# Six conditioning units computed on VectorE inside the feed-forward, weight slabs split two at a time there, pairs of PSUM banks that start even

## The reference

```python
for i in range(DEPTH_2):
    mod = (cond @ ada_w[i] + ada_b[i])[:, None, :]
    shift1, scale1, gate1, shift2, scale2, gate2 = jnp.split(mod, 6, axis=-1)
    h = rmsnorm(x, norm1_g[i]) * (1.0 + scale1) + shift1
    ...
    x = x + gate1 * y
    h = rmsnorm(x, norm2_g[i]) * (1.0 + scale2) + shift2
    x = x + gate2 * swiglu(h, f_w_in[i], f_w_out[i])
```

## Time and profile before

| what | us |
|---|---|
| median of 3 runs (1325.82 to 1327.03) | 1325.92 |
| the profiled execution | 1325.81 |
| its span (first to last instruction) | 1324.0 |
| PE busy in the span | 1137.3 (86%) |
| DVE busy | 633.5 (48%) |
| ACT busy | 547.1 (41%) |

### The profile page before, as it was taken

The page is one execution under the profiler, slowest core; times in us unless marked ns, Lnnn a source line. Parts: engine busy times, 40 slices in busy tenths (PEclk is TensorE's granted clock), DMA queues, the critical chain, the costliest instruction groups (busy, mean ns, idle before and its releaser), DMA issues.

```text
span 1324.0 us, 20070 instructions
## 1 busy us (share of the span) xinstructions
PE 1137.3 (86%) x8573; PEld 843.4 (64%) x8573; DVE 633.5 (48%) x1331; ACT 547.1 (41%) x1185; POOL 0.2 (0%) x4
## 2 busy tenths in 40 slices
PE   6999999867665765756799989999999989999997
PEld 4777667534343442424467758788887758888886
DVE  4565765111111011101175765776666765776665
ACT  4554554111011111101155664666654654666653
POOL 0000000000000000000000000000000000000000
PEclk9999999999798897879999999999999999999999
DMA  9996947999999999999998645654546555655400
GB/s 390 421 425 246 386 160 296 429 427 426 427 425 426 427 426 425 428 427 426 426 403 327 253 192 195 251 191 191 191 159 249 226 224 199 246 191 191 191 32 32
DMA packets 29703, 397.37 MB, mean 300 GB/s; under 512 B 3496, under 2 KB 4904, under 8 KB 5416
## 3 DMA queue, kind: packets, MB, share of 16 engines
q1 hardware_dynamic: 29176, 395.72, 73.5%
q10 hardware_dynamic: 432, 0.30, 0.1%
HBM read 394.97 MB, written 1.05 MB: 299 GB/s over the span
## 4 chain that ended last, share of the span: by engine, by line
PE 61%; DMA 23%; DVE 9%; ACT 6%; issue 1%; SPq 0%; DVEq 0%; ACTq 0%
PE ps L1140 16%; DMA ring<-in_w13b 12%; PE ps L1141 8%; DMA mem<-in_w13b 6%; PE ps L1132 5%; PE ps L1134 5%; PE ps L1133 5%; PE ps L1173 4%; DMA ring<-in_w 4%; PE ps L1643 3%; ACT mem L1815 3%; PE ps L1603 2%; DVE memr L2309 2%; PE ps L1698 2%; ACT memr L1815 2%; DVE mem L2309 2%
## 5 line engine op out<-in xcount | busy, mean ns | idle before, releaser
L2309 DVE TENSOR_TENSOR memr<-ring,memr 128x512 fp32r<-128x512 f32 x432 | 294.2, 690 | 207.2 <-ACT memr L1815 201.2
L1815 ACT ACTIVATE memr<-ring 128x512 fp32r<-128x512 f32 x432 | 266.0, 628 | 197.4 <-PE ps L1141 99.2
L1140 PE MATMUL ps<-memr 128*128 128x512 f32 x952 | 339.1, 399 | 2.8 <-DVE memr L2315 1.8
L1815 ACT ACTIVATE mem<-ps 128x512 f32<-128x512 f32 (+5 forms) x307 | 128.4, 439 | 402.1 <-PE ps L1643 231.6
L1141 PE MATMUL ps<-memr 128*128 128x256 f32 x952 | 267.3, 281 | 0.0
L1140 PEld LDWEIGHTS ps<-memr 128*128 128x128 f32 x952 | 178.9, 188 | 47.9 <-DVE memr L2315 5.9
L1132 PE MATMUL ps<-memr 128*128 128x256 f32 (+2 forms) x504 | 178.8, 355 | 6.8 <-DVE memr L2309 3.9
L1141 PEld LDWEIGHTS ps<-memr 128*128 128x128 f32 x952 | 179.9, 189 | 1.7
L1134 PE MATMUL ps<-memr 128*128 128x256 f32 (+2 forms) x504 | 165.4, 328 | 0.0
L1133 PE MATMUL ps<-memr 128*128 128x256 f32 (+2 forms) x504 | 165.2, 328 | 0.0
L2309 DVE TENSOR_TENSOR mem<-mem,ps 128x512 f32<-128x512 f32 (+1 forms) x76 | 43.5, 572 | 243.1 <-ACT mem L1815 243.0
(11 more groups left out here) (180 smaller groups left out, 1086.2 us busy)
## 6 DMA issues: line engine op xcount, KB each, us to landing
ring<-in_wpk SPq DMA_DIRECT2D x89, 2048.0 KB, 8.2
ring<-in_w13a SPq DMA_DIRECT2D x17, 2048.0 KB, 45.3
mem<-in_w13b SPq DMA_DIRECT2D x16, 2048.0 KB, 45.3
ring<-in_w SPq DMA_DIRECT2D x16, 2048.0 KB, 45.7
ring<-in_w13b SPq DMA_DIRECT2D x16, 2048.0 KB, 43.6
mem<-in_w13a SPq DMA_DIRECT2D x15, 2048.0 KB, 45.3
mem<-in_w SPq DMA_DIRECT2D x15, 2048.0 KB, 46.3
mem<-in_wpk SPq DMA_DIRECT2D x1, 2048.0 KB, 11.2
```

Source lines behind the costliest of these rows:

```text
L1140: te.matmul(ps[:, 0:512], a[0], b[1], start=start, stop=False)
L1815: return self.e.activation(out, src, f, **k)
L2309: return self.e.tensor_tensor(out, a, b, op)
```

## The change

1. Six units, `TURNED` = (1,10), (2,2), (2,3), (2,6), (2,7), (2,8), are taken off PE. Their weights are laid out turned on the host, so that `turned_chunk` computes 128 columns of the unit in one DVE operation: a scalar_tensor_tensor of 128 x 1024 that multiplies the weights with `m.cond` (silu(c) in all partitions) and writes the sum over each row into `m.mcol`. Four chunks make a unit, `turned_end` adds the bias. The generator `turned_units` is put into `p.side` ahead of layer 2's feed-forward and issues one chunk every five slab steps: 24 chunks over 116 of the 132 steps of that feed-forward.
2. `spread_cond` makes `m.cond` once among the experts: eight small PE matmuls and two ACT copies. `m.cond` takes the place of some constants and of `rowb[:, 0]`, so from group 4 on only z = 1 is used.
3. The six units are loaded between the units of layer 2's feed-forward (`TURNED_AT`), no more in the attention phases. Group 7 is now (2,4), (2,5); it is complete before layer 3 begins and is copied in the third step of its modulation.
4. In both feed-forwards `p.at_once = 2` during the 11 blocks: `stage` waits until two of the four places are free, and splits two slabs with one ACT and one DVE operation of 1024 columns.
5. `take_pair` only takes pairs of banks that start with an even one.
6. `warm(9)` is added between the first two modulation units.

```diff
@@ -95,8 +95,10 @@
        ((0, 10), (0, 11), (1, 0), (1, 1), (1, 2), (1, 3)),
-       ((1, 4), (1, 5), (1, 6), (1, 7)), ((1, 8), (1, 9), (1, 10), (2, 2), (2, 3)), ((1, 11), (2, 0), (2, 1)),
-       ((2, 4), (2, 5), (2, 6), (2, 7), (2, 8)), ((2, 9),), ((2, 10), (2, 11)))
+       ((1, 4), (1, 5), (1, 6), (1, 7)), ((1, 8), (1, 9)), ((1, 11), (2, 0), (2, 1)),
+       ((2, 4), (2, 5)), ((2, 9),), ((2, 10), (2, 11)))
+TURNED_AT = (0, 2, 4, 6, 8, 11)
+TURNED = ((1, 10), (2, 2), (2, 3), (2, 6), (2, 7), (2, 8))
 ADA_AT = {u: (g, r) for g, units in enumerate(ADA) for r, u in enumerate(units)}
@@ -246,12 +248,13 @@
         self.cols = sb("cols", [128, CN])
-        self.cst = sb("cst", [128, KN])
+        self.cst = sb("cst", [128, KN + 1024])
         self.w40 = sb("w40", [128, NK, 40])
         self.am = sb("am", [128, 3, 2, 8])
-        self.rowb = sb("rowb", [128, 2, 512])
+        self.rowb = self.cst[:, KN:KN + 1024].rearrange("p (a b) -> p a b", a=2)
+        self.cond = self.cst[:, KN - 512:KN + 512]
         self.csb = sb("csb", [128, 2, NK, 31 + ADA_MOST])
@@ -410,14 +413,16 @@
     mixed((U_AQKV, 8), ada(1, 4), (U_AQKV + 2, 8), ada(1, 5), (U_AQKV + 4, 8), ada(1, 6), ada(1, 7),
-          (U_AQKV + 1, 8), ada(1, 8), (U_AQKV + 3, 8), ada(2, 2), (U_AQKV + 5, 8), ada(2, 3),
-          (U_AWO, 8), ada(1, 9), ada(1, 10), (U_AWO + 1, 8), ada(1, 11), ada(2, 0), ada(2, 1))
+          (U_AQKV + 1, 8), ada(1, 8), (U_AQKV + 3, 8), (U_AQKV + 5, 8),
+          (U_AWO, 8), ada(1, 9), (U_AWO + 1, 8), ada(1, 11), ada(2, 0), ada(2, 1))
     for i in range(2):
-        mixed(*[(U_FIN + 11 * i + n, 8) for n in range(11)],
-              *[(U_FOUT + 6 * i + n, 8 if n < 5 else 4) for n in range(6)])
+        for n in range(17):
+            packed(*((U_FIN + 11 * i + n, 8) if n < 11 else (U_FOUT + 6 * i + n - 11, 8 if n < 16 else 4)))
+            if i == 0 and n in TURNED_AT:
+                packed(*ada(*TURNED[TURNED_AT.index(n)]))
         if i == 0:
-            mixed(ada(2, 4), ada(2, 5), (U_BQKV, 8), (U_BQKV + 2, 8), (U_BQKV + 1, 8), (U_BWO, 8), ada(2, 6), ada(2, 7),
-                  ada(2, 8), (U_BWO + 1, 8), ada(2, 9), ada(2, 10), ada(2, 11))
+            mixed(ada(2, 4), ada(2, 5), (U_BQKV, 8), (U_BQKV + 2, 8), (U_BQKV + 1, 8), (U_BWO, 8),
+                  (U_BWO + 1, 8), ada(2, 9), ada(2, 10), ada(2, 11))
     return units, dense, moe_last
@@ -479,15 +485,15 @@
     def stage(self, most=NSP):
-        most += self.made
-        while not self.hold and self.made < min(len(self.slabs), most) and self.made < self.spent + NSP:
+        most = min(len(self.slabs), most + self.made)
+        while not self.hold and self.made + self.at_once <= min(most, self.spent + NSP):
             n, j = self.slabs[self.made]
             k = self.made
-            self.made += 1
+            self.made += self.at_once
             self.split(k, n, j)
-            if j == self.dense[n][-1]:
+            if j + self.at_once - 1 == self.dense[n][-1]:
                 self.load_unit(self.slot_of[n], (self.s.dve_low, k))
@@ -550,7 +556,9 @@
             g, last = self.ada_made.pop(0)
-            z = self.ada_n % 2
+            z = 1 if g >= 4 else self.ada_n % 2
+            if g >= 4:
+                self.ada_close(True)
             self.ada_n += 1
@@ -568,6 +576,22 @@
+    def turned_units(self):
+        for i, n in TURNED:
+            u = self.unit()
+            self.in_use.remove(u)
+            for c in range(4):
+                self.turned_chunk(i, n, c, u)
+                if c < 3:
+                    for _ in range(5):
+                        yield
+            self.turned_end(i, n)
+            self.ada_done.add((i, n))
+            self.load_unit(self.slot_of[u], (self.s.dve_mod, (i, n)))
+            for _ in range(5):
+                yield
@@ -755,6 +779,7 @@
         self.extra_end()
+        self.spread_cond()
         self.next_gather(GUARD + 1)
@@ -881,16 +906,13 @@
         qk_unit("q11", 2, 0.125, m.qT1, 1, self.a_free)
-        self.ada_unit(2, 2)
         qk_unit("k11", 0, 1.0, m.kT1, 1, self.turned("q10"))
-        self.ada_unit(2, 3)
         self.side.append(self.paced(at, [4, 0, 0, 0]))
         self.ada_unit(1, 9)
-        self.ada_unit(1, 10)
         self.side.append(self.paced(at, [0] * 9))
@@ -911,10 +933,7 @@
         last = self.last
-        self.ada_mm(2, 6)
         self.drain()
-        self.ada_copy()
-        self.ada_close(True)
         last_q = self.chain(*[rope("q21", m.qst2[1][:, tt, :], 4, 0, tt, 4 + tt) for tt in range(2)])
@@ -924,10 +943,6 @@
             next(last_q, None)
-            if step in (1, 4):
-                self.ada_unit(2, 7 if step == 1 else 8)
-            if step == 6:
-                self.ada_close(True)
         self.side.append(self.paced(at, [0] * 8))
@@ -945,6 +960,7 @@
     p.ada_copy()
+    p.warm(9)
     p.ada_mm(0, 2)
@@ -1062,6 +1078,9 @@
         p.modulate_x(i, 1, ("m", i), {3: p.ada_copy})
+        if i == 1:
+            p.side.append(p.turned_units())
+        p.at_once = 2
         for n in range(11):
@@ -1070,6 +1089,7 @@
         p.h2_free = [(s.pe_slab, p.last)]
+        p.at_once = 1
         p.norm_open(("f", i))
@@ -1105,7 +1125,7 @@
         at = {b[0]: j for j, b in enumerate(self.banks)}
-        i = min((i for i in range(7) if i in at and i + 1 in at), key=lambda i: (max(at[i], at[i + 1]), i))
+        i = min((i for i in range(0, 8, 2) if i in at and i + 1 in at), key=lambda i: (max(at[i], at[i + 1]), i))
         freed = [dict(self.banks)[i + z] for z in range(2)]
@@ -1172,6 +1192,20 @@
+    def spread_cond(self):
+        te, w, s, m = self.e, self.w, self.s, self.m
+        for h in range(2):
+            b = self.take(("cond", h))
+            w.wait_ge(s.dve_cond, 1)
+            w.wait_ge(s.ld_c1, "c1")
+            self.ready(b)
+            for k in range(4):
+                c = m.csb[:, 1, 4 * h + k, ADA_MOST - 1:ADA_MOST].to_broadcast([128, 128])
+                r = te.matmul(b.ps[:, 128 * k:128 * k + 128], c, m.ident, start=True, stop=True)
+            r.then_inc(*s.pe_ada.up(("cond", h)))
+            self.give(("cond", h), (s.act_row, ("cond", h)))
@@ -1836,11 +1870,21 @@
         w.wait_ge(self.ring(n), n)
-        for f in self.split_free[k % NSP]:
-            w.wait_ge(*f)
-        self.act(m.sp[:, k % NSP, 0, :], self.slot(n)[:, 512 * j:512 * j + 512]).then_inc(*s.act_high.up(k))
+        z, a = k % NSP, self.at_once
+        for q in range(a):
+            for f in self.split_free[z + q]:
+                w.wait_ge(*f)
+        self.act(m.sp[:, z:z + a, 0, :], self.slot(n)[:, 512 * j:512 * (j + a)].rearrange("p (a n) -> p a n", a=a)
+                 ).then_inc(*s.act_high.up(*range(k, k + a)))
+    def spread_cond(self):
+        w, s, m = self.w, self.s, self.m
+        for h in range(2):
+            w.wait_ge(s.pe_ada, ("cond", h))
+            self.act(m.cond[:, 512 * h:512 * h + 512], m.of(("cond", h))[:, :]).then_inc(*s.act_row.up(("cond", h)))
+        self.row_free = [(), ()]
@@ -2331,10 +2375,10 @@
         w, s, m = self.w, self.s, self.m
-        z = k % NSP
+        z, a = k % NSP, self.at_once
         w.wait_ge(s.act_high, k)
-        self.tt(m.sp[:, z, 1, :], self.slot(n)[:, 512 * j:512 * j + 512], m.sp[:, z, 0, :], ALU.subtract
-                ).then_inc(*s.dve_low.up(k))
+        self.tt(m.sp[:, z:z + a, 1, :], self.slot(n)[:, 512 * j:512 * (j + a)].rearrange("p (a n) -> p a n", a=a),
+                m.sp[:, z:z + a, 0, :], ALU.subtract).then_inc(*s.dve_low.up(*range(k, k + a)))
@@ -2351,6 +2395,20 @@
+    def turned_chunk(self, i, n, c, u):
+        w, s, m = self.w, self.s, self.m
+        v = self.slot(u)[:, 1024 * c:1024 * c + 1024]
+        w.wait_ge(self.ring(u), u)
+        w.wait_ge(s.act_row, ("cond", 1))
+        self.e.scalar_tensor_tensor(out=v, in0=v, scalar=1.0, in1=m.cond, op0=ALU.mult, op1=ALU.mult,
+                                    accum_out=m.mcol[:, i, 4 * n + c:4 * n + c + 1]).then_inc(*s.dve_mod.up(("chunk", i, n)))
+    def turned_end(self, i, n):
+        w, s, m = self.w, self.s, self.m
+        mc = m.mcol[:, i, 4 * n:4 * n + 4]
+        w.wait_ge(s.dve_mod, ("chunk", i, n))
+        self.tt(mc, mc, m.cols[:, C_ADA + 48 * i + 4 * n:C_ADA + 48 * i + 4 * n + 4], ALU.add).then_inc(*s.dve_mod.up((i, n)))
```

More of the change, by code:

```diff
@@ L48 @@
 K_ID, K_ONE, K_INV, K1 = 0, 128, 256, 320
-K_M3, K_MT, K_U, K_BD, K_HS, K_IO = 320, 704, 832, 960, 1088, 1600
-K_CA, K_SA, K_CRC, K_SRC = 1632, 1664, 1696, 1952
+K_M3, K_MT, K_U, K_BD, K_IO = 320, 704, 832, 960, 1088
+K_CA, K_SA, K_CRC, K_SRC, K_HS = 1120, 1152, 1184, 1440, 1696
 KN = 2208
@@ L440, in __init__ @@
         self.hold = False
+        self.at_once = 1
         self.side, self.jobs = [], []
@@ L697 @@
     first_loads = late_loads = cond = rope_tables = first_norm = pad_conv = nothing
-    ada_product = ada_row = ada_turn = ada_gain = nothing
+    ada_product = ada_row = ada_turn = ada_gain = turned_chunk = turned_end = spread_cond = nothing
```

(6 more changed lines are left out.)

## The result

The changed kernel takes 1357.33 us (median of 5), the kernel before 1325.82 in the same session: ratio 1.0238, 95% interval 1.0227 to 1.025. It is slower, as forecast, but by 31.5 us and not by 21.9, and 0.3 us beyond the end of the range.

What follows compares the result with a forecast made beforehand. PE was taken to set the pace in the feed-forwards, chains of waits in attention. Terms -7.8 + 0.5 - 0.4 + 21.0 + 2.5 + 0.8 + 5.3 = +21.9 on 1325.81 gave 1347.7 us, range 1334 to 1357.

Steps and rivals of the forecast that it cites:

- term 3: Slabs in pairs in both feed-forwards: +21.0 us for waits in the blocks, +2.5 at their starts, +0.8 for `norm_tables`.
- term 4: The 24 chunks on DVE in layer 2's feed-forward: 1.30 us each, four of them costly, +5.3 us in all.
- term 1: Six modulation units off PE, mostly in attention: -7.8 us, of which (2,2) and (2,3) 3.7 and (1,10) 1.8.
- the walk: Step-by-step timing of one feed-forward block's ACT and DVE queues with pairs: PE waits 0.40, then 0.66 us.
- Two slabs ahead are enough: Rival, feed-forward blocks: the waits and the chunks' costs vanish, so it ends faster at 1320.6 us; chance 0.10.
- That is 1.05 us a block: Added PE wait per block with pairs, for ten blocks in each of two layers: 21.0 us.
- Start of the feed-forward: First pair comes later behind modulation on ACT and DVE: 1.6 us in layer 2, 0.95 in layer 3, sum 2.5.
- layer 3's +0.95: At the start of layer 3's feed-forward, slab 4 as half of a pair comes 0.95 us later.
- The clock rival: Holes in PE's work in the blocks halve the clock for a tenth of 361 us: +36, 1384 us; chance 0.03.
- The six in `fold_out` [...] 0: Six of the 24 chunks fall into `fold_out`, meet single splits with 2.9 us in hand and cost 0.
- no gain in attention: Rival: in attention another wait takes the removed units' place, so 7.8 us is not gained, 1355.5 us; chance 0.10.
- Term 2: What moves: group 7's copy +0.5 us, loads under the feed-forward hidden, `spread_cond` 0, even bank pairs 0, `warm(9)` -0.4.

Runs made afterwards that it cites:

- Experiment 2: The kernel before with only the slab pairs (`at_once`) in both feed-forwards, no chunks, odd bank pairs allowed; 1.0222 of the kernel before.
- 3: The changed kernel with two places still released together, but each split by its own ACT and DVE operation of 512 columns; 1.0032 of the kernel before.
- 4: The changed kernel with wide pairs, the later parts of `hidden` moved behind the pairs in the queues; 1331.43 us, 1.0036 of the kernel before.
- 5: The changed kernel with silu's table load moved from the first `hidden` to slab 5 of the first block; 1.0225 of the kernel before.
- 8: The changed kernel with single splits and units (2,2) and (2,3) back on PE, four turned units left; 0.9985 of the kernel before.
- 9: The changed kernel with single splits and without the nine idle matmuls `warm(9)` at the start; 0.9979 of the kernel before.
- experiment 11: The changed kernel with `hidden`'s later parts behind pairs, chunks after slabs 2 and 5, early table load, pairs from slab 4 of the first block; 1321.76 us, 0.9968.
- number 6: The changed kernel with the first chunk, and so all 24, three slab steps later; 1.0224 of the kernel before.

## Why the prediction was right in kind and short in size

The direction and the main mechanism were right; the sum was 9.6 us short. What failed are terms of the sum: the block in term 3 was put too low, the table load and the half clock were put at nothing, the last chunks of term 4 were put at nothing, and units (2,2) and (2,3) in term 1 were put at their full PE time. Experiment 2 shows that the pairs lose the time by themselves, 3 that the width of the operations and not the release in twos does it, 4 that it is the order in the two queues, and the steady block above follows the walk operation by operation. "Two slabs ahead are enough" is shown false for this order, and true for the order of 4 where there are no chunks (layer 3). Point by point:

- **Term 3, the block.** "That is 1.05 us a block" was mis-sized: 1.20 (12.49 against 11.29). The two waits are 0.45 and 0.60, in sum as walked (0.40 and 0.66). I left out that the first matmul pair after a wait takes 0.45 instead of 0.354, twice a block; 0.05 comes back as the pairs between the waits stand 0.347 apart. 20 blocks: 3.0 us too little.
- **Term 3, `hidden` at the first block.** The walk had no table load. Before, it lay in the 2.9 us of slack; with pairs it costs 0.8 in each layer, shown by 5: 1.6.
- **Start of the feed-forward.** The hole was as summed (0.51 + 1.6 = 2.1), and layer 3's +0.95 came as forecast. But I held the clock safe because attention keeps 1.00 with 79% busy; a busy share over 20 us says nothing about one hole. The clock rival came true for some 3 us, and that cost 1.6: this is the difference to number 5, which has the same hole at full clock. Whether such a hole brings the half clock differs from run to run, so this term is in part chance.
- **Term 4.** The chunk's 1.30 and its four costly places were right (extra 1.2 to 1.3 in those blocks), `norm_tables` too (0.8 in number 2). "The six in `fold_out` [...] 0" was wrong: the one after slab 2 of the second matrix delays the last product, and PE waits 0.88 at 981.62. The start of `fold_out` gives 1.1 in all.
- **Term 1.** (1,10) gave its 1.8 (1.9 from (1,9) to (2,1)). (2,2) and (2,3) gave 1.2 where I put 3.7, shown by 8: 2.5 too much. PE busy before and after a unit does not mean that nobody else needed the pause. This is the rival "no gain in attention" for two of the six units. Layer 3's attention came as forecast in sum, and I did not test its parts.
- **Term 2.** `warm(9)` gives nothing that can be told (9). Loads under the feed-forward and `spread_cond` left no trace in the stage times; they were not tried alone.

3.0 + 1.6 + 1.6 + 1.1 + 2.5 is 9.8; the miss is 9.6. All five go one way. The table load, the hole at the start and the late chunk are things that fit into slack before and not after; the restart behind a wait exists only with waits; and (2,2) and (2,3) had covered waits of others. The range was also narrower than its own terms: the walk's bounds allow 15.4 a layer, 9.8 more than the sum used, which by itself gives 1357.5.

## What to carry to other kernels

When work is handed out in larger pieces, look at the time until the first part can be used, and at what stands ahead of it in each in-order queue; average load says little, and here both helping engines became less busy in the blocks while the blocks became slower. When a change takes slack away, list everything that lived in that slack (table loads, small set-up operations, the restart of an engine), not only the steady state. If a wide operation is wanted, first move the chained operations behind it: in layer 3 the same two wide splits cost 1.2 us a block in one order and nothing in the other. And price two changes together as well as apart: here the chunks cost 1.4 us alone and 8.0 beside the pairs.

## What was not expected of the hardware

The distance of matmul pairs in the stream has two values, 0.347 and 0.353 us, and a block takes 11.10 or 11.29 by it. With wide splits and no waits it is nearly always 0.347 (every block of layer 3 in experiment 11, nine of the ten after the first in 4, one of them with the table load on top). With single splits it is nearly always 0.353. But neither is tied to the width: single blocks of layer 2 in experiments 8 and 9 take 11.11 with single splits, one of layer 3 in 4 takes 11.30 with wide ones, and the changed kernel has 0.353 ahead of its first wait and 0.347 behind it. What decides is left open.

A hole of some 2 us in PE's work costs more than its length in four of six cases (number 6). In layer 2's attention the granted clock falls once in most of these runs, at 770 to 800, at slightly different places, and moves a stretch of 62.5 us by up to 0.9.
